# Final norm of a streaming encoder step: VectorE takes the mean of the next tile ahead of the scaling of this one

## The chip, the cores and the metric

The kernel runs on one core of one Trainium2 chip. The metric is the device time of one execution in microseconds (us). The engines are named as the profile names them: PE is TensorE (PEld its weight loads), DVE is VectorE, ACT is ScalarE, POOL is GpSimd, SP is SyncE, which here only starts transfers. Each engine works through its own list of instructions in order, and engines wait for each other on semaphores.

## The reference, cut to what matters

The reference is one inference step of one encoder layer (a mixer of three head groups, then a mixture of 16 experts) over 512 frames of a new stream and 64 frames of a running one, model width 1024. The change touches its last operation alone, the RMS norm of the finished rows:

```
def rms_norm(x, w):
    xf = x.astype(F32)
    y = xf * lax.rsqrt(jnp.mean(xf * xf, axis=-1, keepdims=True) + EPS) * w.astype(F32)
    return y.astype(x.dtype)
...
    y_prompt = rms_norm(xp, final_norm_w)
    y_sample = rms_norm(xs, final_norm_w)
```

## The kernel before

The 576 rows are five tiles: four of 128 rows and one of 64 (`NT` is 5, `ROWS` gives their rows, `T0` their first row). Everything ahead of the final norm is the same before and after: projections, attention, the two scans, the output projection, the router, and the experts, whose weighted outputs POOL adds into the rows in HBM (`x_rows`) with one indirect transfer for each expert. When the last of these has landed, SP loads the five finished tiles back into SBUF (line 925, `x_out(i)`, a slice of the old weight buffer, so the trace calls it `weight_ring`). Then, for each tile i, four engines take turns:

- ACT squares the tile and sums each row (`squares`, line 1211, an ACTIVATE and a short ACTIVATION_READ_ACCUMULATOR; its unused output goes to `mixT`). It raises `final_sq`.
- DVE turns the 128 sums into mean + eps (`mean`, line 1504, 128x1). It raises `final_mean`.
- POOL raises that to the power -0.5 (`inv_rms`, line 1067, 128x1). It raises `final_rms`. The sums, means and roots lie in columns of one tile, `small`.
- DVE multiplies the tile by the root of its row and by the norm weight, in place (line 2000, a SCALAR_TENSOR_TENSOR whose two tensor inputs, the tile and `wfb`, named `final_b`, lie in SBUF). It raises `y_normed`.
- ACT starts the store of the tile to the output (line 1205).

Nothing but the order in which each engine's list was written and the semaphores sets the order of the work. ACT's list already runs one tile ahead: it squares tile i, then waits for `y_normed` of tile i-1 and starts that tile's store, then squares tile i+1:

```
            for i in range(NT + 1):
                if i < NT:
                    r = ROWS[i]
                    act.wait_ge(S(f"x_out{i}_in"), 16)
                    squares(i, r, x_out(i).rearrange("p (a b) -> p a b", a=2), mixT[0:r, 0:2, 0:512], "final_sq")
                if i >= 1:
                    n = i - 1
                    r = ROWS[n]
                    act.wait_ge(S("y_normed"), n + 1)
```

POOL's list holds the five roots one after the other, each waiting only for its mean. DVE's list before the change finishes one tile (mean, wait for the root, scaling) before it takes the next.

Of the kernel before, what the change touches and what calls it, by code (L numbers as in the profile page):

```python
# [28 lines left out]
def encoder_layer(nc, ins, outs):  # L29
# [5 lines left out]
    D = x_prompt.shape[2]  # L35
    SEQ, DEC = x_prompt.shape[1], x_sample.shape[1]
    KD = D // P
    NT = SEQ // P + 1
    TOK = SEQ + DEC
    ROWS = [P] * (NT - 1) + [DEC]  # L40
# [5 lines left out]
    HC, PC, NS = state_ssm.shape[2:]  # L46
    TAPS, CH = conv_w.shape[1:]
    NE, _, FE = exp_gate.shape[1:]
    NG = rg_w.shape[2]
    EG = NE // NG  # L50
# [23 lines left out]
    with ExitStack() as ctx:  # L74
        sems = {}

        def S(name):
            if name not in sems:
                sems[name] = ctx.enter_context(nc.semaphore(name))
            return sems[name]  # L80
# [3 lines left out]
        def sb(name, shape, dt=F32, at=None):  # L84
            size = int(np.prod(shape[1:])) * mybir.dt.size(dt)
            size += (-size) % 32
            if at is None:
                at = place[0]
                place[0] += size
            return nc.alloc_sbuf_tensor_at(name, shape, dt, offset=base + at), at, at + size  # L90
# [4 lines left out]
        SLOT_W = 532  # L95
        NSLOT = 3
        wring, _, _ = sb("weight_ring", [P, NSLOT, KD * SLOT_W])
        down, down_at, down_end = sb("down_ring", [P, 2, FE // P * D])
        ident, _, _ = sb("ident", [P, P])
        triu, _, _ = sb("triu", [P, P])  # L100
        striu, _, _ = sb("striu", [P, P])
# [82 lines left out]
        wfb, _, e = sb("final_b", [P, D], at=e)  # L184
# [39 lines left out]
        A_SSQ, A_MS, A_RS, A_MH = 0, 8, 16, 24  # L224
# [53 lines left out]
        def x_out(i):  # L278

            return wring[:, :, :].rearrange("p s c -> p (s c)")[0:ROWS[i], i * D:(i + 1) * D]  # L280
# [39 lines left out]
        def nkeys(i):  # L320
            return T0[i] + P if i < NT - 1 else PAST + DEC
# [1169 lines left out]
        def _(dve):  # L1491
            v = nc.vector
# [7 lines left out]
            def col(c, n=1, rows=P):  # L1500
                return small[0:rows, c:c + n]

            def mean(ssq, ms, n, rows, over, sem):
                v.tensor_scalar(col(ms, n, rows), col(ssq, n, rows), 1.0 / over, EPS, ALU.mult, ALU.add).then_inc(S(sem), 1)  # L1504

            for n in range(NT + 2):
# [5 lines left out]
                i = n - 2  # L1512
                if i >= 0:
                    r = ROWS[i]
# [87 lines left out]
            for j in range(4):  # L1602
# [10 lines left out]
                for t in range(1, TAPS):  # L1613
                    ins = v.scalar_tensor_tensor(out=acc, in0=xpre[:, j, t:t + L], scalar=tap(t), in1=acc,
                                                 op0=ALU.mult, op1=ALU.add)
# [15 lines left out]
            for i in range(NT):  # L1631
                r = ROWS[i]
# [83 lines left out]
                for h in range(HC):  # L1716
# [3 lines left out]
                                                 in1=o[g * NS:(g + 1) * NS, h * PC:(h + 1) * PC], op0=ALU.mult, op1=ALU.add)  # L1720
# [23 lines left out]
                for h in range(HB):  # L1744
                    p0, p1 = h * DK, (h + 1) * DK
                    ins = v.scalar_tensor_tensor(out=Sg[p0:p1, seq(i), h, :], in0=Sg[p0:p1, seq(i), h, :],
                                                 scalar=small[p0:p1, A_EBL:A_EBL + 1], in1=o[p0:p1, h * DV:(h + 1) * DV],
                                                 op0=ALU.mult, op1=ALU.add)
# [69 lines left out]
            for n in range(HEADS):  # L1818
                p, second = divmod(n, 2)
                if not second and p < NT * PAIRS:  # L1820
                    i, j = divmod(p, PAIRS)
                    r, nk = ROWS[i], nkeys(i)
# [17 lines left out]
                for i, step in steps_behind(n):  # L1840
                    r = ROWS[i]
# [48 lines left out]
            for k, a_ in ((R_K1, R_A1), (R_K2, R_A2)):  # L1890
# [13 lines left out]
                                        op0=ALU.add, op1=ALU.mult))  # L1904
# [87 lines left out]
            dve.nop()  # L1992


            def final(i):
                r = ROWS[i]
                dve.wait_ge(S("final_sq"), i + 1)
                mean(A_SSQ + i, A_MS + i, 1, r, D, "final_mean")
                dve.wait_ge(S("final_rms"), i + 1)
                v.scalar_tensor_tensor(out=x_out(i), in0=x_out(i), scalar=col(A_RS + i, 1, r),  # L2000
                                       in1=wfb[0:r, :], op0=ALU.mult, op1=ALU.mult).then_inc(S("y_normed"), 1)

            for i in range(NT):
                final(i)


_INS = ['x_prompt', 'x_sample', 'cache_k_a', 'cache_v_a', 'state_gla', 'state_conv', 'state_ssm', 'norm1_w', 'w_in',
# [31 lines left out]
```

## Time and profile before

| | |
|---|---|
| median of 3 runs | 657.87 us (656.5 to 658.4) |
| profiled execution, its own time | 659.01 us |
| span of its core in the profile | 657.3 us, so 1.7 us lie around it |
| PE busy | 578.9 us (88%) |
| DVE busy | 267.1 us (41%) |
| ACT busy | 166.5 us (25%) |
| POOL busy | 114.2 us (17%) |

The busy shares are means over the whole span. PE carries nearly all of it, but the change lies in the last 15 us, where PE has no work, so these shares tell nothing about it; only the rows of that stretch do.

### The profile page before, as it was taken

The numbers are of one execution on the slowest core, as the hardware profiler recorded it, in microseconds if no ns is written. First come the engines' busy times: TensorE is split into PE (matmuls) and PEld (weight loads), VectorE is DVE, ScalarE is ACT, GpSimd is POOL, SyncE is SP. The second block draws the span as 40 slices with busy tenths as digits, with TensorE's granted clock in tenths as the row PEclk, the third lists the DMA queues.
The fourth block names the chain that finished last, engine by engine and source line by source line (L and its number), as shares of the span: only waits on it lengthen the run. The fifth ranks groups of instructions, "written<-read, shape, count | busy, mean of one in ns | idle before, by whom it ended". The sixth has DMA issues, their size and how long they took to land.

```text
span 657.3 us, 7139 instructions
## 1 busy us (share of the span) xinstructions
PE 578.9 (88%) x2430; PEld 326.2 (50%) x2430; DVE 267.1 (41%) x767; ACT 166.5 (25%) x451; POOL 114.2 (17%) x152
## 2 busy tenths in 40 slices
PE   2999999999999998999999998379999999998930
PEld 2786765537777753335555655334443443443310
DVE  1601466666666645344555532532122222121104
ACT  5202253232323222234444321011111111111113
POOL 4000004232323221000000000163122122121011
PEclk9999999999999999999999999569999999999975
DMA  7923032011011030505112044713999999999837
GB/s 246 328 73 129 0 129 65 1 55 73 1 55 74 1 129 19 200 17 201 41 64 85 14 145 154 262 37 90 332 327 313 299 325 314 298 312 297 240 58 277
DMA packets 63994, 99.94 MB, mean 152 GB/s; under 512 B 10365, under 2 KB 43312, under 8 KB 63926
## 3 DMA queue, kind: packets, MB, share of 16 engines
q1 hardware_dynamic: 53306, 75.90, 34.3%
q0 software_dynamic: 4576, 13.40, 8.9%
q10 hardware_dynamic: 6076, 10.19, 4.3%
q8 instruction: 20, 0.33, 0.2%
q14 instruction: 16, 0.13, 0.1%
HBM read 85.01 MB, written 17.08 MB: 155 GB/s over the span
## 4 chain that ended last, share of the span: by engine, by line
PE 42%; DMA 11%; issue 5%; DVE 4%; SPq 2%; POOL 1%; ACT 1%; POOLq 0%; DVEq 0%
PE bank L855 11%; PE bank L761 9%; DMA weight_ring<-in_exp_w_up 8%; PE bank L871 7%; PE bank L494 4%; PE bank L706 2%; PE bank L725 2%; SPq L925 2%; PE bank L689 2%; PE bank L841 1%; PE bank L783 1%; DMA x_rows<-expert_y,router_index 1%; DVE weight_ring L2000 1%; POOL small L1067 1%; DMA expert_x<-h_rows,router_index 1%
## 5 line engine op out<-in xcount | busy, mean ns | idle before, releaser
L855 PE MATMUL bank<-weight_ring,expert_xT 128*96 128x512 f32 x256 | 116.9, 608 | 7.2 <-DMA weight_ring<-in_exp_w_up 6.1
L855 PEld LDWEIGHTS bank<-weight_ring,expert_xT 128*96 128x96 f32 x256 | 40.9, 166 | 72.1 <-issue 60.6
L482 PE MATMUL bank<-hT,weight_ring 128*128 128x288 f32 x256 | 69.9, 410 | 0.0
L761 PE MATMUL bank<-weight_ring,mixT 128*128 128x512 f32 x128 | 60.0, 602 | 0.0
L871 PE MATMUL bank<-down_ring,expert_hiddenT 128*96 128x512 f32 x128 | 58.8, 602 | 0.9 <-ACT expert_hiddenT L1435 0.9
L1067 POOL TENSOR_TENSOR small<-small 128x1 f32<-128x1 f32 (+5 forms) x25 | 16.7, 674 | 206.1 <-DVE small L1504 206.1
L482 PEld LDWEIGHTS bank<-hT,weight_ring 128*128 128x128 f32 x256 | 47.0, 190 | 10.9 <-issue 0.5
L1970 DVE TENSOR_TENSOR expert_hidden<-bank,expert_silu 96x256 f32<-96x256 f32 x16 | 6.7, 421 | 106.7 <-ACT expert_silu L1431 106.7
L399 PE MATMUL bank<-hT,weight_ring 128*128 128x288 f32 x192 | 47.6, 408 | 1.1 <-ACT gla_v L1237 0.7
L399 PEld LDWEIGHTS bank<-hT,weight_ring 128*128 128x128 f32 x192 | 36.2, 190 | 11.7 <-issue 2.0
L1431 ACT ACTIVATE expert_silu<-bank 96x256 f32<-96x256 f32 x16 | 6.1, 379 | 139.2 <-PE bank L855 139.2
L494 PE MATMUL bank<-weight_ring,hT 128*128 128x512 f32 (+1 forms) x80 | 39.4, 611 | 0.0
L1148 POOL DMA_INDIRECT x_rows<-expert_y,router_index x16 | 25.1, 1571 | 77.1 <-DVE router_index L1928 37.7
L469 PE MATMUL bank<-weight_ring,hT 128*128 128x512 f32 (+1 forms) x80 | 38.5, 598 | 0.0
L871 PEld LDWEIGHTS bank<-down_ring,expert_hiddenT 128*96 128x96 f32 x128 | 19.6, 162 | 27.5 <-issue 25.5
L761 PEld LDWEIGHTS bank<-weight_ring,mixT 128*128 128x128 f32 x128 | 22.5, 190 | 21.2 <-issue 20.6
L1983 DVE TENSOR_SCALAR expert_y<-bank,slot_weight 96x512 f32<-96x512 f32 x16 | 11.9, 747 | 49.7 <-PE bank L871 49.7
L1094 POOL TENSOR_TENSOR gla_q_decayed<-gla_q_blocks,gla_exponents 128x256 f32<-128x256 f32 (+1 forms) x34 | 24.5, 727 | 43.5 <-issue 23.5
L1136 POOL DMA_INDIRECT expert_x<-h_rows,router_index x16 | 15.8, 988 | 88.8 <-PE bank L841 73.8
L1830 DVE TENSOR_TENSOR bank<-bank,att_bias 128x256 f32<-128x256 f32 (+1 forms) x32 | 12.6, 394 | 30.1 <-PE bank L689 30.0
L563 PE MATMUL bank<-gla_q_decayed,gla_k_decayed 128*128 128x256 f32 (+1 forms) x68 | 20.0, 376 | 4.1 <-POOL gla_q_decayed L1094 4.0
L1395 ACT ACTIVATE att_pT<-bank 128x128 f32<-128x128 f32 (+3 forms) x40 | 14.4, 401 | 34.9 <-PE bank L706 34.9
(315 smaller groups left out, 793.5 us busy)
## 6 DMA issues: line engine op xcount, KB each, us to landing
weight_ring<-in_exp_w_gate SPq DMA_DIRECT2D x32, 512.0 KB, 9.5
weight_ring<-in_exp_w_up SPq DMA_DIRECT2D x32, 512.0 KB, 10.8
down_ring<-in_exp_w_down SPq DMA_DIRECT2D x16, 1024.0 KB, 6.4
weight_ring<-in_w_in SPq DMA_DIRECT2D x5, 2048.0 KB, 8.5
weight_ring<-in_w_out SPq DMA_DIRECT2D x2, 2048.0 KB, 8.4
weight_ring<-in_w_in SPq DMA_DIRECT2D x1, 2112.0 KB, 12.3
x_rows<-x ACTq DMA_DIRECT2D x4, 512.0 KB, 2.6
h_rows<-h ACTq DMA_DIRECT2D x4, 512.0 KB, 2.6
```

The lines of the kernel that those rows point to most:

```text
L399: last = mm(bank[b][0:m, 0:HALF], w[:, k, c0:c0 + m], hT[:, k, half], start=(k == 0), stop=(k == KD - 1))
L469: last = mm(o[0:ROWS[i], :], hT[:, k, T0[i]:T0[i] + ROWS[i]], w[:, k, :], start=(k == 0), stop=(k == KD - 1))
L482: last = mm(o[:, 0:HALF], w[:, k, j * P:(j + 1) * P], hT[:, k, half], start=(k == 0), stop=(k == KD - 1))
L494: last = mm(o[0:ROWS[i], :], hT[:, k, T0[i]:T0[i] + ROWS[i]], w[:, k, :], start=(k == 0), stop=(k == KD - 1))
L563: last = mm(o[0:r, 0:HB * r // 2], kE[:, c % 2, 0:r], qE[:, c % 2, :, 0:r // 2], start=True, stop=True)
L761: last = mm(bank[3][0:ROWS[i], 0:512], mixT[:, k, T0[i]:T0[i] + ROWS[i]], ring(G_WO0 + hf, 512)[:, k, :], start=(k == 0), stop=(k == KD - 1))
L855: last = mm(o[0:CAP, :], xgT[:, e % 2, k, :], w[:, k], start=(k == 0), stop=(k == KD - 1))
L871: last = mm(o[0:CAP, :], hidT[:, e % 2, j, :], down[:, e % 2, j * D + hf * 512:j * D + (hf + 1) * 512], start=(j == 0), stop=(j == FE // P ...
L1067: g.tensor_tensor(small[0:rows, out:out + n], small[0:rows, col:col + n], small[0:rows, A_MH:A_MH + n], ALU.pow).then_inc(S(sem), 1)
L1094: g.tensor_tensor(qE[:, c % 2, :, 0:r // 2].rearrange("p h (n m) -> p h n m", m=m), later(qbd[:, :, 0:r], m), e_.unsqueeze(1).broadcast_to ...
L1136: g.indirect_dma_start(out=xg[0:CAP, e % 2, :], out_offset=None, in_=h2_d, in_offset=bass.IndirectOffsetOnAxis(ap=ri[0:CAP, 16 + e:17 + e] ...
L1148: g.indirect_dma_start(out=x1_d, out_offset=bass.IndirectOffsetOnAxis(ap=ri[0:CAP, 16 + e:17 + e].bitcast(U32), axis=0), in_=ye[0:CAP, e % ...
```

## The change

On DVE, the mean of tile i+1 now stands ahead of the scaling of tile i. Its loop has one round more; round i takes the mean of tile i (if there is one) and then waits for the root of tile i-1 and scales that tile. The instructions are the same ten, with the same shapes, and the lists of the other engines are the same.

```diff
-            def final(i):
-                r = ROWS[i]
-                dve.wait_ge(S("final_sq"), i + 1)
-                mean(A_SSQ + i, A_MS + i, 1, r, D, "final_mean")
-                dve.wait_ge(S("final_rms"), i + 1)
-                v.scalar_tensor_tensor(out=x_out(i), in0=x_out(i), scalar=col(A_RS + i, 1, r),
-                                       in1=wfb[0:r, :], op0=ALU.mult, op1=ALU.mult).then_inc(S("y_normed"), 1)
-
-            for i in range(NT):
-                final(i)
+            for i in range(NT + 1):
+                if i < NT:
+                    dve.wait_ge(S("final_sq"), i + 1)
+                    mean(A_SSQ + i, A_MS + i, 1, ROWS[i], D, "final_mean")
+                if i >= 1:
+                    n = i - 1
+                    dve.wait_ge(S("final_rms"), n + 1)
+                    v.scalar_tensor_tensor(out=x_out(n), in0=x_out(n), scalar=col(A_RS + n, 1, ROWS[n]),
+                                           in1=wfb[0:ROWS[n], :], op0=ALU.mult, op1=ALU.mult).then_inc(S("y_normed"), 1)
```

The end of DVE's list, before (-) and after (+): L1504 is the mean, L2000 and L2002 the scaling, `small` holds the sums, means and roots, `weight_ring` is the tile, `final_b` the norm weight.

```order
+L1504 TENSOR_SCALAR small<-small 128x1 x2
+L2002 SCALAR_TENSOR_TENSOR weight_ring<-weight_ring,small,final_b 128x1024
 L1504 TENSOR_SCALAR small<-small 128x1
-L2000 SCALAR_TENSOR_TENSOR weight_ring<-weight_ring,small,final_b 128x1024
+L2002 SCALAR_TENSOR_TENSOR weight_ring<-weight_ring,small,final_b 128x1024
 L1504 TENSOR_SCALAR small<-small 128x1
```

Two means now stand ahead of the first scaling, and from there a mean of tile i+1 stands ahead of each scaling of tile i; the last two scalings follow each other.

The end of ACT's list, the same before and after: L1211 is `squares` of a tile, L1205 the start of a store of one.

```order
L1211 ACTIVATE mixT,small<-weight_ring 128x2x512 x2
L1205 DMA out<-weight_ring 128x1024
L1211 ACTIVATE mixT,small<-weight_ring 128x2x512
L1205 DMA out<-weight_ring 128x1024
L1211 ACTIVATE mixT,small<-weight_ring 128x2x512
L1205 DMA out<-weight_ring 128x1024
```

Nothing moved here: the squares of tile i+2 stand behind the store of tile i, and that store waits for the scaling of tile i.

## Rows read from the trace of the kernel before

**Rows 1.** The page: PE and DVE busy, in tenths, in 40 slices of the span.

```profile
PE   2999999999999998999999998379999999998930
...
DVE  1601466666666645344555532532122222121104
```

**Rows 2.** The chain that ended last, from 633 us: start us, us, what.

```profile
633.69 5.19 DMA x_rows<-expert_y,router_index
...
638.89 3.68 DMA weight_ring<-x_rows
...
642.60 1.16 ACT mixT L1211 x2
```

**Rows 3.** Timeline of the final norm: start us, us, engine, line, operation [idle before <-releaser].

```profile
643.56 0.19 ACT L1211 ACTIVATION_READ_ACCUMULATOR mixT<-weight_ring 128x1 f32 x1
643.78 0.15 DVE L1504 TENSOR_SCALAR small<-small 128x1 f32<-128x1 f32 x1 [12.32 <-ACT mixT L1211]
...
644.63 1.28 DVE L2000 SCALAR_TENSOR_TENSOR weight_ring<-weight_ring,small,final_b 128x1024 f32<-128x1024 f32 x1 [0.70 <-POOL small L1067]
644.82 0.19 ACT L1211 ACTIVATION_READ_ACCUMULATOR mixT<-weight_ring 128x1 f32 x1
645.84 0.15 DVE L1504 TENSOR_SCALAR small<-small 128x1 f32<-128x1 f32 x1
645.95 0.35 ACTq L1205 DMA_DIRECT2D out<-weight_ring  x1
646.06 0.55 POOL L1067 TENSOR_TENSOR small<-small 128x1 f32<-128x1 f32 x1 [1.46 <-DVE small L1504]
646.41 1.06 ACT L1211 ACTIVATE mixT<-weight_ring 128x1024 f32<-128x1024 f32 x1 [1.41 <-DVE weight_ring L2000]
646.64 1.28 DVE L2000 SCALAR_TENSOR_TENSOR weight_ring<-weight_ring,small,final_b 128x1024 f32<-128x1024 f32 x1 [0.66 <-POOL small L1067]
647.37 0.19 ACT L1211 ACTIVATION_READ_ACCUMULATOR mixT<-weight_ring 128x1 f32 x1
...
652.09 0.54 POOL L1067 TENSOR_TENSOR small<-small 64x1 f32<-64x1 f32 x1 [1.45 <-DVE small L1504]
652.66 1.27 DVE L2000 SCALAR_TENSOR_TENSOR weight_ring<-weight_ring,small,final_b 64x1024 f32<-64x1024 f32 x1 [0.66 <-POOL small L1067]
```

**Rows 4.** Who waited for whom, 636 to 658 us: total us, times, longest.

```profile
ACT mixT L1211 <- DMA weight_ring<-x_rows: 12.9, 1, 12.9
...
DVE weight_ring L2000 <- POOL small L1067: 3.3, 5, 0.7
ACT mixT L1211 <- DVE weight_ring L2000: 3.1, 3, 1.4
```

**Rows 5.** Timeline at 127 us: a mean of four columns and the operation behind it.

```profile
127.13 0.17 DVE L1504 TENSOR_SCALAR small<-small 128x4 f32<-128x4 f32 x1
127.21 0.26 DVE L1746 SCALAR_TENSOR_TENSOR gla_state<-gla_state,small,bank 32x64 f32<-32x64 f32 x1
```

**Rows 6.** Timeline at 28 us: two short DVE operations on different tiles.

```profile
28.41 0.15 DVE L1544 TENSOR_SCALAR small<-small 128x4 f32<-128x4 f32 x1
28.59 0.18 DVE L1546 TENSOR_SCALAR params_T<-params_T 128x20 f32<-128x20 f32 x1
```

**Rows 7.** Timeline at 119 us, and line 1105 by form (min/median/max ns).

```profile
119.21 0.42 DVE L1706 TENSOR_TENSOR ssd_decay<-ssd_decay,ssd_cb 128x256 f32<-128x256 f32 x1
119.26 0.85 POOL L1105 TENSOR_TENSOR ssd_x_w<-xB_nat,small 128x256 f32<-128x256 f32 x1 [2.04 <-DVE small L1702]
...
L1105 POOL TENSOR_TENSOR ssd_x_dt<-xB_nat,small x5: 605/612/613, 116.0 to 245.4; 128x256 f32<-128x256 f32 x4, 64x256 f32<-64x256 f32 x1
...
L1105 POOL TENSOR_TENSOR ssd_x_w<-xB_nat,small x5: 712/851/852, 119.3 to 248.7; 128x256 f32<-128x256 f32 x4, 64x256 f32<-64x256 f32 x1
```

**Rows 8.** Windows: us, busy time and count of PE, PEld, DVE, ACT, POOL, PEclk, DMA share, GB/s.

```profile
653.94:657.30 3.36, 0.00 (x0) 0.00 (x0) 0.00 (x0) 0.00 (x0) 0.00 (x0) 0.50 0.40 96
```

**Rows 9.** Transfers from 630 us on: KB each, median us from issue to landing.

```profile
out<-weight_ring ACTq DMA_DIRECT2D x1, 256.0 KB, 2.9
```

## The prediction

> **What bounds the kernel now.** I began with the page's strip of 40 slices [rows 1]: PE is at nine tenths almost to the end and at zero in the last slice, where DVE is at four tenths. So the end of the program is a stretch in which PE has nothing left, and the change lies wholly in it. The chain that ended last says what that stretch hangs on [rows 2]: the last indirect transfer of the experts (633.69 us), the load of the finished rows (638.89) and the squares (642.60); the timeline [rows 3] shows the mean, the root and one scaling after another behind them. Every microsecond that this chain gains or loses is one of the run, since nothing runs beside it that ends later. That timeline and the waits [rows 4] then say how a tile is passed from engine to engine. One period runs from the scaling of tile 0 at 644.63 to that of tile 1 at 646.64, 2.01 us, and four of them lead to the last scaling at 652.66 (8.03 us in all). A period is 1.28 us of scaling and about 0.7 us in which DVE waits for POOL's root, five times, 3.3 us in all. This wait is what the change goes for. The other row of that view matters as much: ACT waits for DVE's scaling three times, 3.1 us. In the timeline ACT starts a store 0.04 us after a scaling ends (645.91 to 645.95) and the next squares only behind that, at 646.41. So squares of tile i+2 never start ahead of the end of the scaling of tile i. Before the change that wait costs nothing: the squares are done at 647.56, ahead of the end of the scaling beside them at 647.92.
>
> **What the change does to that loop.** Nothing is added or removed: ten DVE operations in another order, no transfer more or less. But DVE works in order, and the scaling of tile i now stands behind the mean of tile i+1, which needs the squares of tile i+1. Those start, from i = 1 on, only after the scaling of tile i-1. What ran side by side (squares of tile i+2 under the scaling of tile i+1) becomes one ring: scaling, store, squares, mean, next scaling. What is queued behind the waiting mean is the scaling itself, and for the scaling wait ACT's store and, behind it, the next squares.
>
> The period of the ring, from [rows 3] unless another group is named:
> - scaling 1.28 us;
> - end of scaling to start of squares: 645.91 to 646.41, 0.50 us (it holds the start of the store);
> - squares with the reading of their sums: 646.41 to 647.56, 1.15 us;
> - end of squares to start of the mean: 643.75 to 643.78, 0.03 us;
> - start of the mean to start of the scaling behind it, whose root is long there: the trace has no such pair in this loop. The nearest is a mean followed by an unrelated operation of the same kind, 127.13 to 127.21, 0.08 us [rows 5]; the other end is a pair spaced at 28.41 and 28.59, 0.18 us [rows 6]. I take 0.08, since the form and its neighbour are those of [rows 5].
>
> The sum is 1.28 + 0.50 + 1.15 + 0.03 + 0.08 = 3.04 us, against 2.01.
>
> The start moves too. The squares of tile 1 end at 645.01 (644.82 + 0.19), so the mean of tile 1 starts at 645.04 and the first scaling at 645.12 instead of 644.63. Three periods later the fourth scaling starts at 645.12 + 9.12 = 654.24 and ends at 655.52. The fifth needs no further squares, since the mean of tile 4 is already taken. With nothing else in its way it would start as the fourth ends.
>
> **The root under the scaling.** Here one thing stands in the way. POOL's root of tile i+1 is started by the mean, and its record begins 0.22 us after the mean's (645.84 to 646.06), while the scaling begins 0.08 us after it. So the root now meets a DVE operation that reads two tiles in SBUF. A root by POOL under exactly such a scaling isn't in the trace. What is: at 119.21 a DVE product of two SBUF tiles runs for 0.42 us, and a POOL product that begins at 119.26 takes 0.85 us instead of 0.61 [rows 7]; it ends 0.48 us after DVE's. The five of that form take 0.85 us in the median and none under 0.71, five others of that line 0.61. So POOL seems to stand still until DVE is done, except for its first 0.13 us or so (0.61 - 0.48). By that the root, 0.54 us long, ends 0.41 us after the scaling (0.54 - 0.13).
>
> The Trainium skill, "SBUF — State Buffer", section "SBUF: two separate sides", says the same thing more strictly: VectorE with two SBUF inputs and GpSimd share one pair of ports, the first to start has it for its whole instruction, and the other is blocked; further down it adds about 115 ns after VectorE's end. The trace agrees that POOL is held; it has 0.48 us left of 0.61, which is less than a whole instruction. By the page the last scaling would start 0.69 us after the one ahead of it (0.115 + 0.54 + 0.03), and the run come out 0.25 us above what I sum below.
>
> For tiles 1 to 3 a late root costs nothing. It is there about 0.4 us after the scaling, and the next scaling comes 1.76 us after it (0.50 + 1.15 + 0.03 + 0.08). For tile 4 it is the end of the chain: the last scaling starts 0.41 + 0.03 us after the fourth ends (0.03 is the step from root to scaling, 652.63 to 652.66). Bounds: not held at all, 0 us; held for its whole length, 0.57 us.
>
> **The sum.** The fifth scaling starts at 655.52 + 0.44 = 655.96 and, 1.27 us long, ends at 657.23. Before it ended at 653.93. That is 3.30 us later. What follows stays: 3.36 us from there to the span's end [rows 8], the store of the last tile, which lands 2.9 us after its issue [rows 9], and what ends the program. The store of tile 3 is issued 1.71 us ahead of it (about 2.0 before), so the two overlap a little more than now; I put this at nothing. Loads take no part: ACT waited for them once, for the first tile [rows 4], and each later tile is asked for no sooner than before. So the profiled execution goes from 659.01 to about 662.3 us. The median of the runs shown is 1.1 us below that execution, and from 657.87 the same step gives **661.2 us**, 0.5% slower.
>
> Bounds of the step: with the root not held 2.86 us; with it held whole and 0.18 us from mean to scaling at all four places, 3.30 + 0.13 + 0.40 = 3.83 us. A single run of before stands up to 1.4 us off the median, a median of three less, some 0.7 us.
>
> **The rivals.**
> - *The root isn't held.* Then the last scaling starts as the fourth ends, at 655.52, and the end moves by 2.86 us: 660.7. For it speaks that a root reads only two columns and may have read them within its first moments. Against it: the product in [rows 7] lost time though it began only 0.05 us into DVE's.
> - *The root gets in first and holds the scaling.* If the mean releases POOL sooner than DVE can start the scaling, the scaling waits out the root, up to 0.54 us less what is past, say 0.4 us at each of four tiles. The period is 3.44 us, the fifth scaling comes at once after the fourth, and the end moves by 2.86 + 1.6 = 4.5 us: 662.3. It decides where the step from mean to scaling passes the 0.22 us to POOL's record; both bounds that I have, 0.08 and 0.18, are under it.
> - *The other side: the wait goes and nothing takes its place.* If ACT's squares could run ahead, the scalings would follow each other at 1.28 + 0.08 us, the first at 645.12; the fifth would end at 645.12 + 4 x 1.36 + 1.27 = 651.83, 2.1 us earlier than now: 655.8. This needs squares of tile i+2 that don't wait for the scaling of tile i. It turns to a gain where they end at least 1.03 us sooner after that scaling (3.04 less 2.01) than the ring has them. For it speaks only that the 3.3 us of waiting are real. Against it speaks the wait of ACT in [rows 4], and that each squares of the last three tiles starts behind a store.
> - *No change to see.* It would take a term of the ring that shrinks by half a microsecond or more at each tile, such as squares or scaling made faster once they no longer run side by side. The first squares run alone, beside no scaling, and take 1.15 us like the later ones (643.56 + 0.19 ends 1.15 us after 642.60 in [rows 2]). So I see no room: within 2 us of 657.9.
>
> **How the numbers follow.** A difference of about 0.3%, 2.0 us, is what a measurement of this kernel can tell from no change. Chances: forecast (ring with the root held, 660.3 to 662.0) 0.65; root not held 0.12; root first 0.09; gain 0.05; no change 0.05; something else 0.04. The first three are all slower by over 0.3% in their middle, but the smallest step, 2.86 us, less a run's scatter, can fall under 2.0, so some of it goes to "same". Slower 0.87, same 0.08, faster 0.05. The range for 8 in 10 takes in the first two cases with the scatter and reaches to the middle of the third: 659.5 to 662.4 us.
>
> **What would show it.** In the new profile the means should stand ahead of the scalings, the first scaling 0.49 us later behind the first squares than now, and four scalings 3.04 us apart. DVE's wait should no longer be for POOL but for ACT's squares, about 1.7 us at each of three tiles. The roots should be recorded at about 1.5 us instead of 0.55 if they are held (1.14 us to the end of the scaling, then 0.41), and DVE should wait for POOL once, about 0.4 us, ahead of the last scaling. Scalings of 1.7 us beside roots of 0.55 would show the second rival. I am wrong at the root if squares of tile 2 start ahead of the end of the first scaling, or if the scalings come closer than 2 us apart.

## The result, and the profile after

The changed kernel takes 658.34 us (median of 22 runs, 654.96 to 663.56). The kernel before, run beside it, takes 654.29 us (22 runs, the three shown ahead among them, 651.09 to 658.4). The ratio is 1.0058, with a 95% interval of 1.0036 to 1.0080: slower by 2.4 to 5.2 us. The forecast was slower by 3.30 us (0.5%), which lies inside that interval. The forecast of the time was 661.2 us, with a range of 659.5 to 662.4; the measured 658.34 lies below that range. The forecast was built on a level of 657.87 us, and the kernel before runs at 654.29.

The timeline of the changed kernel's final norm answers to [rows 3] (start us, us, engine, line, operation, idle before and what ended it). L2002 is the scaling.

```profile
641.43 1.06 ACT L1211 ACTIVATE mixT<-weight_ring 128x1024 f32<-128x1024 f32 x1 [13.12 <-DMA weight_ring<-x_rows]
...
643.87 0.15 DVE L1504 TENSOR_SCALAR small<-small 128x1 f32<-128x1 f32 x1 [1.11 <-ACT mixT L1211]
643.95 1.28 DVE L2002 SCALAR_TENSOR_TENSOR weight_ring<-weight_ring,small,final_b 128x1024 f32<-128x1024 f32 x1
644.11 1.52 POOL L1067 TENSOR_TENSOR small<-small 128x1 f32<-128x1 f32 x1 [0.67 <-DVE small L1504]
645.25 0.35 ACTq L1205 DMA_DIRECT2D out<-weight_ring  x1
645.71 1.06 ACT L1211 ACTIVATE mixT<-weight_ring 128x1024 f32<-128x1024 f32 x1 [1.87 <-DVE weight_ring L2002]
...
646.89 0.15 DVE L1504 TENSOR_SCALAR small<-small 128x1 f32<-128x1 f32 x1 [1.67 <-ACT mixT L1211]
646.96 1.28 DVE L2002 SCALAR_TENSOR_TENSOR weight_ring<-weight_ring,small,final_b 128x1024 f32<-128x1024 f32 x1
...
652.96 1.27 DVE L2002 SCALAR_TENSOR_TENSOR weight_ring<-weight_ring,small,final_b 128x1024 f32<-128x1024 f32 x1
653.12 1.52 POOL L1067 TENSOR_TENSOR small<-small 64x1 f32<-64x1 f32 x1 [1.47 <-DVE small L1504]
...
654.67 1.28 DVE L2002 SCALAR_TENSOR_TENSOR weight_ring<-weight_ring,small,final_b 64x1024 f32<-64x1024 f32 x1 [0.44 <-POOL small L1067]
```

Read it from the waits in square brackets. Before, each scaling waited for POOL. Now the means of tiles 2 to 4 wait 1.65 to 1.67 us for ACT's squares, those squares wait 1.85 to 1.87 us for DVE's scaling, and the scaling follows its mean at once, without a wait: the ring. Scalings stand 3.01 us apart (643.95 to 646.96), where they stood 2.01 us apart. Each root that runs under a scaling has a record of 1.52 us instead of 0.55, and the last scaling waits 0.44 us for the last of them.

The same view that [rows 4] come from, for the changed kernel (who waited for whom: us in total, times, longest):

```profile
DVE small L1504 <- ACT mixT L1211: 18.6, 5, 12.5
...
ACT mixT L1211 <- DVE weight_ring L2002: 5.6, 3, 1.9
DVE weight_ring L2002 <- POOL small L1067: 0.4, 1, 0.4
```

DVE's wait for POOL fell from 3.3 us to 0.4, as the change meant it to. In its place DVE waits for ACT at all five means (12.5 us of it is the wait for the first tile, which was there before), and ACT's wait for DVE grew from 3.1 us to 5.6.

I measure the final norm from the start of the squares of tile 0. To the end of the last scaling it was 11.33 us (642.60 to 653.93) and is 14.52 us (641.43 to 655.95); to the span's end it was 14.7 us and is 17.9. So either grew by 3.2 us, while the span of the profile grew only from 657.3 to 659.4: this execution reached the final norm 1.2 us sooner, in code that the change leaves as it is.

### The profile page after: what moved, and what is told of

It is laid out like the page before. It is cut to its first block, busy times and chain, and to the rows that moved or that the text cites. A ratio compares the mean times of both kernels' runs of the same rounds, so it can differ in the third digit from the quotient of the medians.

```text
span 659.4 us, 7139 instructions
## 1 busy us (share of the span) xinstructions
PE 579.0 (88%) x2430; PEld 325.2 (49%) x2430; DVE 267.8 (41%) x767; ACT 166.9 (25%) x451; POOL 118.1 (18%) x152
## 4 chain that ended last, share of the span: by engine, by line
PE 43%; DMA 11%; issue 4%; DVE 3%; SPq 2%; ACT 1%; POOL 1%; POOLq 0%; ACTq 0%; DVEq 0%
PE bank L855 11%; PE bank L761 9%; DMA weight_ring<-in_exp_w_up 8%; PE bank L871 6%; PE bank L494 5%; PE bank L706 2%; PE bank L725 2%; PE bank L689 2%; SPq L925 2%; PE bank L841 1%; DMA x_rows<-expert_y,router_index 1%; PE bank L783 1%; DMA weight_ring<-x_rows 1%; DMA expert_x<-h_rows,router_index 1%; POOL small L1067 1%
## 5 line engine op out<-in xcount | busy, mean ns | idle before, releaser
L1067 POOL TENSOR_TENSOR small<-small 128x1 f32<-128x1 f32 (+5 forms) x25 | 20.6, 830 | 204.0 <-DVE small L1504 204.0
```

What stands on the lines that cost most here:

```text
L1067: g.tensor_tensor(small[0:rows, out:out + n], small[0:rows, col:col + n], small[0:rows, A_MH:A_MH + n], ALU.pow).then_inc(S(sem), 1)
```

## The experiments

"The stretch" is the time from the start of the squares of tile 0 to the end of the last scaling. Each run has its ratio to the kernel before with a 95% interval, and its stretch from its trace.

**Cutting the ring.** The changed kernel with ACT's squares of all tiles ahead of its first store:

```diff
-            for i in range(NT + 1):
-                if i < NT:
-                    r = ROWS[i]
-                    act.wait_ge(S(f"x_out{i}_in"), 16)
-                    squares(i, r, x_out(i)...)
-                if i >= 1:
+            for i in range(NT):
+                r = ROWS[i]
+                act.wait_ge(S(f"x_out{i}_in"), 16)
+                squares(i, r, x_out(i)...)
+            for i in range(NT + 1):
+                if i >= 1:
                     n = i - 1
```

> The changed kernel, but ACT squares all five tiles before it waits for a scaling and starts a store. I measure from the start of the squares of tile 0 to the end of the last scaling: 11.33 us before the change (642.60 to 653.93), 14.51 us after it (641.43 to 655.94). Theory (the ring scaling, store, squares, mean, with the root held under the scaling): the ring is cut, the first scaling stays 2.52 us behind the start, and the scalings then follow each other at 1.28 us plus the rest of a held root, 0.44 us, so 1.72 us apart: 2.52 + 4 x 1.72 + 1.28 = 10.7 us, with four waits of DVE for POOL of about 0.44 us. If the ring is right but roots of tiles 1 to 3 are not held, 1.36 us apart: 9.2 us. Rival (the time was lost by the new order on DVE itself or by the stores, not by squares that stand behind a store): it stays within 0.4 us of 14.5 us.

Measured: ratio 1.0006 (0.9984 to 1.0027), so the loss is gone; stretch 11.0 us (638.50 to 649.50). The waits of this run:

```profile
DVE small L1504 <- ACT mixT L1211: 14.6, 4, 11.9
ACT mixT L1211 <- DMA weight_ring<-x_rows: 14.5, 3, 12.5
...
DVE weight_ring L2002 <- POOL small L1067: 0.4, 1, 0.4
```

ACT no longer waits for DVE, and with that wait the ring is gone; DVE's order is still the new one, so the order alone does not cost the time. The size came out near the expected 10.7 us, but not by the expected way: instead of four waits for POOL there is one, and ACT waits for the loads of tiles 2 and 3, 1.42 and 0.53 us. In the kernel before and in the changed one ACT waited for a load only once, for the first tile: by the time that a scaling let it go on, the next tile was there. And to the span's end it took 15.31 us, 0.6 more than before, so what the stretch gained did not reach the end; why is taken up below.

**The same on the old order.** The same edit of ACT on the kernel before, whose DVE order is left alone.

> The kernel before, with ACT's squares of all five tiles ahead of the first store; DVE's order is the old one. Theory: there the squares were never what DVE waited for, so nothing changes: scalings 2.01 us apart, 11.3 us from the first squares to the end of the last scaling (0.2 us either way), time within 0.2% of before. Rival (squares that run ahead are a gain by themselves, whatever DVE's order): the stretch falls below 10.7 us.

Measured: ratio 1.0019 (0.9989 to 1.0050), stretch 11.34 us. The row that sets the pace is the one of before:

```profile
DVE weight_ring L2000 <- POOL small L1067: 3.3, 5, 0.7
```

Squares that run ahead bring nothing by themselves. It takes the new DVE order for squares behind a store to hurt.

**One pair alone.** The kernel before, with only the mean of tile 4 ahead of the scaling of tile 3 (in the list below 0 is a mean, 1 a scaling, then the tile; ... stands for the two branches).

```diff
-            for i in range(NT):
-                final(i)
+            for what, i in ((0, 0), (1, 0), (0, 1), (1, 1), (0, 2), (1, 2), (0, 3), (0, 4), (1, 3), (1, 4)):
+                ...
```

> The kernel before, with one pair of its order changed: the mean of tile 4 stands ahead of the scaling of tile 3, everything else as before. Theory: one turn of the ring and one held root. The scaling of tile 3 waits for the squares of tile 4, which start 0.5 us after the end of the scaling of tile 2: it starts 3.0 us after that one instead of 2.0, so 1.0 us later; the last scaling starts 0.44 us after the fourth ends instead of 0.73, so 0.72 us later than before in all: 12.05 us from the first squares to the end of the last scaling (11.33 before, 14.51 after the change). The root of tile 4 takes 1.52 us, the others 0.55. Rival (the cost sits at the start, or in the order as a whole, and not in each pair): 11.3 us, or more than 13.

Measured: stretch 12.05 us (637.82 to 649.87), as worked out. The ratio, 1.0012 (0.9978 to 1.0047), can't show 0.7 us. The timeline of this run shows the one turn of the ring and the one held root:

```profile
643.88 1.28 DVE L2002 SCALAR_TENSOR_TENSOR weight_ring<-weight_ring,small,final_b 128x1024 f32<-128x1024 f32 x1 [0.66 <-POOL small L1067]
...
646.81 0.15 DVE L1504 TENSOR_SCALAR small<-small 64x1 f32<-64x1 f32 x1 [1.58 <-ACT mixT L1211]
646.88 1.27 DVE L2002 SCALAR_TENSOR_TENSOR weight_ring<-weight_ring,small,final_b 128x1024 f32<-128x1024 f32 x1
647.03 1.52 POOL L1067 TENSOR_TENSOR small<-small 64x1 f32<-64x1 f32 x1 [1.18 <-DVE small L1504]
...
648.59 1.28 DVE L2002 SCALAR_TENSOR_TENSOR weight_ring<-weight_ring,small,final_b 64x1024 f32<-64x1024 f32 x1 [0.44 <-POOL small L1067]
```

The scaling of tile 3 comes 3.00 us after that of tile 2, and the last one 1.71 us behind it instead of 2.0.

**Freeing the root.** The changed kernel, with the norm weight copied to PSUM ahead of the final norm, so that a scaling reads one tensor in SBUF and one in PSUM.

```diff
-        bank = [ctx.enter_context(nc.psum_tensor(f"bank{b}", [P, 512], F32)) for b in range(8)]
+        banks = ctx.enter_context(nc.psum_tensor("bank", [P, 8, 512], F32))
+        bank = [banks[:, b, :] for b in range(8)]
 ...
+            wps = banks[:, 0:2, :].rearrange("p b c -> p (b c)")
+            v.tensor_copy(wps, wfb[:, :]).then_inc(S("final_w_moved"), 1)
+            dve.wait_ge(S("final_w_moved"), 1)
 ...
-                                           in1=wfb[0:ROWS[n], :], ...
+                                           in1=wps[0:ROWS[n], :], ...
```

> The changed kernel, but DVE copies the norm weight into two PSUM banks while it idles ahead of the final norm, and the scaling reads it there: it then reads one tensor in SBUF and one in PSUM. Theory (a root is held because the scaling reads two tensors in SBUF): the roots take 0.55 us again instead of 1.52, the last scaling starts right behind the fourth, 0.43 us sooner, and the ring stays at 3.0 us a tile: 14.1 us from the first squares to the end of the last scaling, against 14.51. Rival (POOL is slowed by any DVE work beside it, or the long record is only how POOL's time is written): roots stay at 1.5 us, or they become short and the last scaling still waits about 0.4 us. A scaling that reads PSUM may itself be some per cent longer; that is then counted apart.

Measured: stretch 13.98 us (641.34 to 655.32), 0.54 us less than the changed kernel's 14.52. The end of its timeline:

```profile
649.87 1.27 DVE L2007 SCALAR_TENSOR_TENSOR weight_ring<-weight_ring,small,bank 128x1024 f32<-128x1024 f32 x1
650.03 0.55 POOL L1068 TENSOR_TENSOR small<-small 128x1 f32<-128x1 f32 x1 [2.45 <-DVE small L1505]
...
652.86 2.46 DVE L2007 SCALAR_TENSOR_TENSOR weight_ring<-weight_ring,small,bank 128x1024 f32<-128x1024 f32 x2
653.01 0.54 POOL L1068 TENSOR_TENSOR small<-small 64x1 f32<-64x1 f32 x1 [2.43 <-DVE small L1505]
```

The roots are back at 0.55 us under a scaling that is as long as ever (1.27), and the last two scalings stand back to back, 2.46 us for both; the ring stays (649.87 to 652.86, 2.99 us). So what holds the root here is that the scaling reads two tensors in SBUF. The time, ratio 1.0065 (1.0032 to 1.0097), is too coarse for half a microsecond.

**Both, and then the stores on another queue.** First the two edits together:

> The changed kernel with both: squares of all tiles ahead of the stores, and the norm weight in PSUM. Theory: neither ring nor held root is left, DVE does a mean and a scaling for each tile back to back, 1.36 us apart: 2.52 + 4 x 1.36 + 1.27 = 9.2 us from the first squares to the end of the last scaling, 2.1 us less than before the change and 5.3 less than after it, if the load of the last tile is in by then. Faster than before by about 0.3%. Rival (roots are held by DVE's work whatever it reads): 10.7 us, as the kernel with squares ahead alone. Rival (the loads of the tiles bound it): gaps of ACT ahead of the squares of tiles 3 and 4, and more than 10 us.

Measured: ratio 0.9997 (0.9974 to 1.0020), stretch 10.27 us (638.95 to 649.22), not 9.2. Its first scaling and first two stores, its waits and its transfers (KB each, median us from issue to landing):

```profile
641.46 1.27 DVE L2007 SCALAR_TENSOR_TENSOR weight_ring<-weight_ring,small,bank 128x1024 f32<-128x1024 f32 x1
...
645.88 0.83 ACTq L1206 DMA_DIRECT2D out<-weight_ring  x2
...
ACT mixT L1212 <- DMA weight_ring<-x_rows: 14.6, 3, 12.9
...
out<-weight_ring ACTq DMA_DIRECT2D x4, 512.0 KB, 4.0
out<-weight_ring ACTq DMA_DIRECT2D x1, 256.0 KB, 4.4
```

The stores of the same size in the kernel before landed sooner:

```profile
out<-weight_ring ACTq DMA_DIRECT2D x4, 512.0 KB, 2.8
```

The second rival of that run is what happened: the loads of tiles 2 and 3 bound it. And what the stretch gained on before, 1.07 us, did not reach the end: from the first squares to the span's end it took 15.15 us, 0.4 us more than before. ACT's stores stand behind the squares that wait for loads; the first store goes out 3.2 us after its scaling (642.73 to 645.88), the five crowd, and they take 4.0 us (median of four) and 4.4 us to land instead of 2.8 and 2.9 [rows 9]. So I moved the stores to SP, which has nothing to do by then, and left ACT the squares alone:

```diff
             for i in range(NT):
                 load(x_out(i), x1_d[T0[i]:T0[i] + ROWS[i], :], f"x_out{i}_in")
+            for n in range(NT):
+                r = ROWS[n]
+                sp.wait_ge(S("y_normed"), n + 1)
+                dst = y_prompt[0, T0[n]:T0[n] + r, :] if n < NT - 1 else y_sample[0]
+                sp.dma_start(dst, x_out(n)).then_inc(S("y_final"), 16)
 ...
```

> The kernel with squares ahead and the norm weight in PSUM, and now SP starts the five stores instead of ACT, so that a store no longer stands behind the squares of later tiles. In the run without this the first store was issued 3.2 us after its scaling had ended, and 4.9 us passed from the end of the last scaling to the end of the span, against 3.4 before. Theory (late, crowded stores took back what the scalings gained): stores go out 0.1 us after each scaling, the end follows the last scaling by 3.4 to 3.6 us, and 13.7 us pass from the first squares to the end of the span, against 15.2 in that run, 14.7 before and 18.0 after the change. Rival (loads and stores share the same bandwidth, so earlier stores only make the loads of tiles 3 and 4 later): ACT waits longer for these loads, and the stretch stays at 14.7 us or more.

Measured: 13.88 us from the first squares to the span's end, 0.9 us less than before and near the 13.7 expected. The ratio was 0.9927 (0.9901 to 0.9954), 4.8 us less, over five times what the trace shows; the trace is of the longest of the ten executions (657.33 us, median 652.17). I ran the same kernel again, and beside it two with only the stores moved:

> The kernel with squares ahead, weight in PSUM and stores on SP once more. Its profile gave 13.88 us from the first squares to the end of the span, 0.9 less than before, but its times a ratio of 0.9927, 4.8 us less. Theory (the rest is the scatter of what comes ahead of the final norm): 13.9 us again, and a ratio nearer to 0.9985, the step of 0.9 us. Rival: 0.993 again, and then something outside the final norm, or runs without a profile, takes part.

> The kernel before with one change: SP starts the stores, so ACT's list holds only the squares there. DVE's old order, norm weight in SBUF. Theory (only the final norm counts, and there the scalings set the pace): scalings 2.01 us apart, 11.3 us from the first squares to the end of the last scaling, 14.8 to the end of the span, time within 0.2% of before. Rival (stores started by SP save time that the profile of the final norm doesn't show, some 3 us in the run with squares ahead, weight in PSUM and stores on SP): a ratio of 0.993 to 0.996 with the same 14.8 us.

> The changed kernel with SP starting the stores, so that no squares stand behind a store; the norm weight stays in SBUF, so roots are held. Theory (the ring needs the store in ACT's list): as with squares ahead, the ring is gone; each scaling follows the held root of the one ahead of it or the load of its tile, 1.7 to 2.6 us apart, 11.0 us from the first squares to the end of the last scaling (14.5 with stores on ACT), roots of 1.5 us, and 3.5 us from there to the end, so 14.5 in all. Rival: the scalings stay 3.0 us apart.

Measured: the same kernel again gave 0.9997 (0.9965 to 1.0028) with 13.04 us to the span's end, 1.7 us less than before (ACT waited 0.42 and 0.72 us for the loads of tiles 2 and 3, where the first set's trace has 1.42 and 0.55). The old order with stores on SP gave 0.9992 (0.9961 to 1.0022) with 14.76 us, no change. The new order with stores on SP gave 1.0006 (0.9972 to 1.0040) with 13.44 us to the end and a stretch of 10.04 us, a microsecond less than the 14.5 and 11.0 expected. Its waits:

```profile
ACT mixT L1216 <- DMA weight_ring<-x_rows: 14.3, 3, 13.3
...
DVE weight_ring L1999 <- POOL small L1072: 0.4, 1, 0.4
```

ACT waits for loads alone: no squares behind a store, no ring, though the scalings still read two tensors in SBUF. Two of the four roots beside a scaling took 1.52 us as expected; the other two took 0.55 and 0.54 (see the last section). So the 0.9927 did not come again, and I don't count it as the kernel's; the two sets ran on two different chips, so whether the chip has a part in it is open. A version that beats the kernel before in time is not shown; in the trace the new order with squares ahead and stores on SP ends 0.9 to 1.7 us sooner than before.

**Both kernels once more.**

> The kernel before itself, as the tried one, to see what its times and its trace scatter by. Theory: the final norm takes the same as in the first trace, 11.3 us from the first squares to the end of the last scaling and 14.7 to the end of the span, within 0.1 us; the difference between executions of up to 4 us lies ahead of it, in the first loads and in the experts; the ratio's interval holds 1 and is some 0.2% to either side. Rival (the final norm itself scatters, and with it the step that the change makes): these stretches differ by 0.5 us or more.

> The changed kernel again. Theory: 14.5 us from the first squares to the end of the last scaling and 18.0 to the end of the span, within 0.1 us, scalings 3.0 us apart, roots of 1.52 us, whatever the time of the whole; the time about 3.3 us above that of before, a ratio of 1.004 to 1.007. Rival: the stretch differs by 0.5 us or more from the first trace of this kernel.

Measured: before against itself 0.9981 (0.9951 to 1.0011), stretch 11.35 us, 14.77 to the end; after 1.0045 (1.0016 to 1.0075), stretch 14.53 us, 17.94 to the end. Both stretches repeat their first trace within 0.02 us. The level does not. Where the loads of the finished rows start tells how late an execution reached the final norm, and the first DVE copy of a projection tells how late it got going. These are rows of three traces: before, the old order with squares ahead, and after once more.

```profile
34.08 0.46 DVE L1549 COPY gla_kT<-bank 128x288 f32<-128x288 f32 x1 [5.31 <-PE bank L399]
638.89 2.31 SPq L925 DMA_DIRECT2D weight_ring<-x_rows  x5
```

```profile
32.30 0.46 DVE L1549 COPY gla_kT<-bank 128x288 f32<-128x288 f32 x1 [5.32 <-PE bank L399]
634.70 2.30 SPq L925 DMA_DIRECT2D weight_ring<-x_rows  x5
```

```profile
640.67 2.35 SPq L925 DMA_DIRECT2D weight_ring<-x_rows  x5
```

Over the 13 traces, in which the work ahead of the final norm is the same, the last loads start between 634.2 and 640.7 us, up to 6.5 us apart, and part of it (1.8 us between the first two) is there in the first 35 us, while the first weights come in.

## Why the prediction was right in its step and wrong in its time

- *The ring.* Forecast 3.04 us a tile, from five terms; measured 3.01. The term taken from farthest off, mean to scaling, was 0.08 as taken from [rows 5] (643.87 to 643.95). Cutting the ring in ACT's list, and turning it once with one pair, show that it is the squares behind the store, together with the mean ahead of the scaling, and neither alone.
- *The start.* First scaling 2.52 us after the first squares, as forecast (645.12 less 642.60).
- *The held root.* Forecast 1.55 us for its record and 0.44 us of wait ahead of the last scaling, from the POOL product in [rows 7]; measured 1.52 and 0.44. The estimate from the Trainium skill's page "SBUF — State Buffer", section "SBUF: two separate sides", was 0.69 us for that wait (its 115 ns come from a transfer that waits for GpSimd). This case agrees that two SBUF inputs of VectorE hold GpSimd; the size is that of the row: the root ended 0.40 us after the scaling (645.63 against 645.23), less than its own 0.55. With the weight in PSUM it isn't held.
- *The step.* Forecast 3.30 us; 3.2 by the stretch. Each of the three periods came out 0.03 to 0.05 us shorter than forecast, which makes up the rest.
- *The rivals.* The root that isn't held, or that gets in first and holds the scaling, did not happen. Squares that run ahead, by an edit of ACT, took the loss away but not the 2.1 us that I gave this rival as its gain: the stretch fell by 0.3 us only, and the end came later. I had left out the held roots, the loads of the later tiles and the crowded stores. With these out of the way the trace gains up to 1.7 us; no gain in time is shown.
- *The step that failed* is the last of the sum: "from 657.87 the same step gives 661.2 us". I took the median of three runs as the level and allowed 0.7 us for it. The level was 654.29 us over 22 runs; the three shown (656.5, 657.87, 658.4) are the first, third and fourth longest of them. 654.29 + 3.30 is 657.6 us, 0.75 under the measured 658.34. So this term was mis-sized by 3.6 us, more than the whole step that I worked out; the mechanism had no part in it. The level itself moves from set to set: in the experiments the kernel before had medians of 655.28, 656.05 and 654.67 us, and beside the 656.05 the changed kernel had 659.56, which falls just inside the range. Nor is the scatter within a set even. In the order of their record the changed kernel's 22 executions alternate: in each of the 11 pairs the first is the longer, by 4.1 us on average (660.5 against 656.5); the same pairing of the kernel before gives 0.9 us. What does that is not known, and it leaves the 4.05 us between the two medians a rougher measure of the step than the 3.2 us of the trace. What makes one execution reach the final norm up to 6.5 us later than another is not settled. The 13 traces place it: PE's 91st matmul starts between 31.8 and 35.7 us, while the first weights come in; from there to its 1711th all take 365.1 us to within 0.1; from there to the last, while the experts' weights stream in, 227.4 to 232.1 us. I tried nothing on either stage.

## What to carry to other kernels

Before you move one engine's work a tile ahead to take away a wait, look at what its producer's list holds between two tiles: if the producer waits for the very result that you now put second, the move closes a ring, and work that ran side by side runs in turn. Move the producer ahead first, or move what blocks it to an idle queue; here either took the loss away, and neither is shown to gain time. And keep a forecast of a step apart from one of a time: with three runs that lie 0.3% apart, the level may still be off by 0.5%.

## What the runs showed that I had not expected

A scaling of two SBUF tensors does not hold every root beside it. With squares ahead and the weight in SBUF, POOL's last root and a scaling began 0.06 us apart with POOL ahead, and both took their usual time:

```profile
646.97 0.54 POOL L1067 TENSOR_TENSOR small<-small 64x1 f32<-64x1 f32 x1
```

```profile
647.03 1.28 DVE L2002 SCALAR_TENSOR_TENSOR weight_ring<-weight_ring,small,final_b 128x1024 f32<-128x1024 f32 x1 [0.39 <-POOL small L1067]
```

In the run with the new order and the stores on SP the last root, 0.07 us ahead of its scaling, went the same way. And there one root began 0.04 us behind its scaling and still was not held:

```profile
647.30 1.30 DVE L1999 SCALAR_TENSOR_TENSOR weight_ring<-weight_ring,small,final_b 128x1024 f32<-128x1024 f32 x1
647.34 0.55 POOL L1072 TENSOR_TENSOR small<-small 128x1 f32<-128x1 f32 x1
```

The roots of 1.52 us and more began 0.13 to 0.16 us behind their scalings, and the product in [rows 7] was held from 0.05 us behind. What becomes of a root that begins between 0.04 and 0.13 us behind was not tried. So the rival in which the root gets in first would have cost next to nothing here (0.02 us at the most in these three), not the 0.4 us a tile that I gave it. And two sets of runs of one and the same kernel gave ratios whose 95% intervals don't meet, 0.9901 to 0.9954 and 0.9965 to 1.0028: such an interval holds the scatter within a set, not what differs between sets, which here includes the chip.
